# A hybrid encoder on one core: the DeltaNet solver's entry reordered, and the norms with spare matmuls, one later POOL unit and halved x transfers

## What is computed

```python
for i in range(DEPTH):                      # DEPTH = 2
    h = _rmsnorm(x, norm_mix[i])
    x = x + (_mixer_gdn if i == 0 else _mixer_ssd)(h, ...)
    x = x + _peer(_rmsnorm(x, norm_ffn[i]), peer_w_q[i], peer_keys[i], peer_u[i], peer_v[i])
return _rmsnorm(x, norm_final)
```

## Time and profile before

| | |
|---|---|
| median of 3 executions | 2225.3 us (2224.41 to 2226.25) |
| the profiled execution: time / span | 2224.22 us / 2222.3 us |
| PE busy | 2145.9 us, 97% of the span |
| DVE / ACT / POOL busy | 67% / 60% / 49% |
| mean granted PE clock | 0.986 |

### The profile page before, as it was taken

How to read it: one execution, slowest core, us unless ns; L and a number is a source line. 1 busy time by engine, 2 the same in 40 slices (tenths; PEclk the granted TensorE clock), 3 DMA queues, 4 the chain that set the end, 5 groups by cost and what they waited for, 6 DMA issues and landing times.

```text
span 2222.3 us, 46035 instructions
## 1 busy us (share of the span) xinstructions
PE 2145.9 (97%) x14384; PEld 1980.1 (89%) x14384; DVE 1488.0 (67%) x3206; ACT 1340.2 (60%) x2739; POOL 1080.7 (49%) x831
## 2 busy tenths in 40 slices
PE   7989799999999999999989998999999999999998
PEld 6979799999999988888888877999999999888886
DVE  5766419975666577777766662399666665777776
ACT  7755455568787544444466775555777875444444
POOL 6841579997667600000066457799866674000000
PEclk9999999999999999999999999999999999999999
DMA  5520245554444566666634225455544445666664
GB/s 170 163 66 1 95 152 171 170 169 150 137 141 142 168 195 191 194 193 191 196 117 159 86 86 171 159 173 161 180 139 137 140 142 174 194 190 196 191 193 145
DMA packets 93872, 343.66 MB, mean 155 GB/s; under 512 B 10688, under 2 KB 10752, under 8 KB 93152
## 3 DMA queue, kind: packets, MB, share of 16 engines
q1 hardware_dynamic: 92592, 338.21, 49.0%
q0 software_dynamic: 912, 4.07, 0.6%
q10 hardware_dynamic: 288, 0.34, 0.1%
HBM read 341.53 MB, written 1.05 MB: 154 GB/s over the span
## 4 chain that ended last, share of the span: by engine, by line
PE 83%; POOL 7%; issue 5%; DVE 2%; ACT 2%; DMA 1%; POOLq 0%; DVEq 0%; ACTq 0%
PE bank L361 81%; POOL w_lo L1796 7%; PE bank L526 1%; PE bank L381 0%; ACT w_hi L1408 0%; DMA small<-in_ssd_d 0%; DVE arena L882 0%; ACT arena L1408 0%; ACT arena L1434 0%; DVE arena L997 0%; DVE arena L1037 0%; DVE arena L1004 0%; DVE arena L933 0%; PE bank L727 0%; PE bank L450 0%
## 5 line engine op out<-in xcount | busy, mean ns | idle before, releaser
L1796 POOL TENSOR_TENSOR w_lo<-ring,w_hi 128x512 fp32r<-128x512 f32 x744 | 996.4, 1355 | 647.3 <-ACT w_hi L1408 635.5
L1408 ACT ACTIVATE w_hi<-ring 128x512 fp32r<-128x512 f32 x1280 | 802.7, 628 | 523.5 <-PE bank L361 521.8
L361 PE MATMUL bank<-hT_hi,w_hi 128*128 128x256 f32 x2688 | 780.2, 290 | 8.4 <-POOL w_lo L1796 6.4
L361 PE MATMUL bank<-hT_lo,w_hi 128*128 128x256 f32 x2688 | 761.5, 283 | 0.0
L361 PE MATMUL bank<-hT_hi,w_lo 128*128 128x256 f32 x2688 | 761.4, 283 | 0.0
L361 PEld LDWEIGHTS bank<-hT_hi,w_hi 128*128 128x128 f32 x2688 | 516.3, 192 | 19.3 <-POOL w_lo L1796 18.7
L361 PEld LDWEIGHTS bank<-hT_lo,w_hi 128*128 128x128 f32 x2688 | 516.8, 192 | 0.0
L361 PEld LDWEIGHTS bank<-hT_hi,w_lo 128*128 128x128 f32 x2688 | 516.0, 192 | 0.0
L908 DVE TENSOR_TENSOR w_lo<-ring,w_hi 128x512 fp32r<-128x512 f32 x536 | 378.4, 706 | 198.7 <-ACT w_hi L1408 191.3
L361 PE MATMUL bank<-w_hi,p_ag_hi 128*128 128x512 f32 x1024 | 398.4, 389 | 0.0
L361 PE MATMUL bank<-w_lo,p_ag_hi 128*128 128x512 f32 x1024 | 398.4, 389 | 0.0
(11 more groups left out here) (250 smaller groups left out, 2252.1 us busy)
## 6 DMA issues: line engine op xcount, KB each, us to landing
ring<-in_peer_u SPq DMA_DIRECT2D x256, 512.0 KB, 3.5
ring<-in_peer_v SPq DMA_DIRECT2D x256, 512.0 KB, 3.7
ring<-in_peer_wq SPq DMA_DIRECT2D x32, 512.0 KB, 3.5
ring<-in_gdn_qkv SPq DMA_DIRECT2D x24, 512.0 KB, 3.5
ring<-in_ssd_xbc SPq DMA_DIRECT2D x24, 512.0 KB, 3.5
ring<-in_ssd_z SPq DMA_DIRECT2D x16, 512.0 KB, 3.6
ring<-in_ssd_out SPq DMA_DIRECT2D x16, 512.0 KB, 3.5
ring<-in_gdn_z SPq DMA_DIRECT2D x8, 512.0 KB, 3.5
```

The lines of the kernel that those rows point to most:

```text
L361: return pe.matmul(o, w, r, start=first, stop=last)
L1408: return act.activation(o, i, ACT.Copy, scale=scale)
L1796: pool.tensor_tensor(w_part[1][:, s, :], ring[:, n % RING, hf * 512:(hf + 1) * 512], w_part[0][:, s, :].bitcast(F32), ALU.subtract).then_i ...
```

## The change

**Solver entry.** The backs move from banks 4 to 7 to banks 2 to 5. The second z half's units no longer stand behind heads 0 to 3: unit 0 stands ahead of the backs, unit 1 behind back 1, unit 2 behind head 5, unit 3 behind head 7. ACT splits two z units between the backs, and the two `go` units in solver steps 8 and 9; its copies of the finished z half move into step 4. POOL makes the rests of the two `go` units after its masks, not before them. DVE runs `extend(0)` behind head 3 and `extend(1)` behind head 5.

**Norms.** In `turn_h(i)` PE makes 18 matmuls of hT with itself into bank 3, whose result nobody reads, before it waits for the first pieces (three float32 matmuls of constants for i = 0). POOL makes the rest of one unit less ahead of the norms 1 and 3 (and of norm 2's unit 1) and waits for the last piece (`n_h`) before that unit; the load of the peer keys moves ahead of that wait. In norm 0 ACT loads the square root's table first.

**Transfers.** x comes in as two DMAs of one token block each, norm 0 takes its squares block by block, and the result goes out as two DMAs, each behind its own scaling.

```diff
@@ sync
-            sp.dma_start(x_sb[:, :, :], a["x"]).then_inc(x_loaded, 16)
+            for t in range(NT):
+                sp.dma_start(x_sb[:, t, :], a["x"][:, t, :]).then_inc(x_loaded[t], 16)
...
+            for t in range(NT):
+                sp.wait_ge(SEM["finished"], t + 1)
+                sp.dma_start(out[:, t, :], x_sb[:, t, :]).then_inc(SEM["stored"], 16)
@@ tensor
             def turn_h(i):
+                for e in range(KEEP_WARM if i else 3):
+                    if i:
+                        mm(PS[3][:, :], hT[0][:, 0, 0:P], hT[0][:, 0:2, :])
+                    else:
+                        mm(PS[3][:, :], ident, const[:, 0:4, :])
                 for b in range(4):
                     pe.wait_ge(n_h, 8 * i + 2 * (b + 1))
...
                 by_token(("gz", 0), 0, 2, 4)
+                pe.wait_ge(row_lo, 1)
+                pe.wait_ge(SEM["g_toksb"], 12)
+                by_token(("gz", 1), 6, 0, 1)
 
                 for gi in range(GH):
                     pe.wait_ge(SEM["g_qk"], gi // 2 + 1)
...
-                            last = pe.transpose(PS[4 + gi % 4][:, (2 * e + t) * P:(2 * e + t + 1) * P],
+                            last = pe.transpose(PS[2 + gi % 4][:, (2 * e + t) * P:(2 * e + t + 1) * P],
                                                 g_tok[:, t, 2 * gi + e, :], ident)
                     last.then_inc(SEM["g_backps"], 1)
+                    if gi == 1:
+                        by_token(("gz", 1), 6, 1, 2)
...
-                    if h < KD // 2:
-                        by_token(("gz", 1), 6, h, h + 1)
+                    if h in (5, 7):
+                        by_token(("gz", 1), 6, (h - 1) // 2, (h + 1) // 2)
@@ vector
-                for h in range(GH):
-                    system_rows(h)
-                dve.wait_ge(SEM["g_exps"], 2)
-                link(dve.tensor_scalar(g_egq, g_eg, P ** -0.5, None, ALU.mult))
...
-                for n in range(GB):
-                    extend(n)
+                for h in range(GH):
+                    system_rows(h)
+                    if h >= 3 and h % 2:
+                        extend((h - 3) // 2)
+                extend(GB - 1)
+                dve.wait_ge(SEM["g_exps"], 2)
+                link(dve.tensor_scalar(g_egq, g_eg, P ** -0.5, None, ALU.mult))
@@ scalar
-                if i:
-
-                    act.activation(n_idle, n_root, ACT.Sqrt)
+                if not i:
+                    act.wait_ge(root_primed, 1)
+                act.activation(n_idle, n_root, ACT.Sqrt)
...
+                    if gi in (3, 6):
+                        split(z + 6 + gi // 6)
...
-                    if h < 4:
-                        split(z + 6 + h)
-                    if h == 5:
-                        z_out(1, 6)
...
                     x_out(n)
+                    if n == GB:
+                        z_out(1, 6)
+                    if n in (2 * GB, 2 * GB + 1):
+                        split(z + n)
@@ gpsimd
             def early_experts(lyr, start):
 
-                rest_of_units(start + 2, tables[lyr] + 2)
+                pool.wait_ge(n_h, 16 * (lyr + 1))
+                rest_of_units(start + 1, tables[lyr] + 2)
...
-            rest_of_units(0, at[("go", 2)])
+            rest_of_units(0, at[("go", 0)])
             for b in range(GB):
                 pool.wait_ge(SEM["g_Ah"], 2 * (b + 1))
...
+            rest_of_units(at[("go", 0)], at[("go", 2)])
...
-            rest_of_units(at[("go", 2)], at[("pq", 0, 0)] + 2)
+            rest_of_units(at[("go", 2)], at[("pq", 0, 0)] + 1)
             load_keys(0)
             early_experts(0, at[("pq", 0, 0)])
```

More of the change, by code:

```diff
@@ L64 @@
 EARLY = 56
+KEEP_WARM = 18
 EXP_AT, TURN_AT = 36, 48
@@ L288, in hybrid_encoder @@
         mask = flat(p_ag[1][:, :, :], "s t")
-        x_loaded, small_loaded, gain_loaded = sem("x_loaded"), sem("small_loaded"), sem("gain_loaded")
+        x_loaded, small_loaded, gain_loaded = [sem(f"x{t}_loaded") for t in range(NT)], sem("small_loaded"), sem("gain_loaded")
+        root_primed = sem("root_primed")
         const_loaded = sem("const_loaded")
@@ L352, in _ @@
             sp.dma_start(last_gain, a["norm_final"].partition_broadcast(P)).then_inc(last_gain_loaded, 16)
-            sp.wait_ge(SEM["finished"], 1)
-            sp.dma_start(out, x_sb[:, :, :]).then_inc(SEM["stored"], 16)
-            sp.wait_ge(SEM["stored"], 16)
+            for t in range(NT):
+                sp.wait_ge(SEM["finished"], t + 1)
+                sp.dma_start(out[:, t, :], x_sb[:, t, :]).then_inc(SEM["stored"], 16)
+            sp.wait_ge(SEM["stored"], 16 * NT)
         @block.tensor
@@ L544, in z_step @@
                     pe.wait_ge(SEM["g_Y"], n - GB + 1)
+                    if n == GB:
+                        pe.wait_ge(SEM["g_zraw"], 2 * NT)
                     if n - 2 >= GB:
@@ L1384, in experts @@
                 residual(n3 - 1)
-            dve.wait_ge(x_loaded, 16)
+            dve.memset(n_root, 1.0).then_inc(root_primed, 1)
+            for t in range(NT):
+                dve.wait_ge(x_loaded[t], 16)
             norm(0)
@@ L1400, in _ @@
             for t in range(NT):
-                ins = dve.scalar_tensor_tensor(x_sb[:, t, :], x_sb[:, t, :], n_rstd[:, t:t + 1], last_gain, ALU.mult, ALU.mult)
-            ins.then_inc(SEM["finished"], 1)
+                dve.scalar_tensor_tensor(x_sb[:, t, :], x_sb[:, t, :], n_rstd[:, t:t + 1], last_gain, ALU.mult, ALU.mult
+                                         ).then_inc(SEM["finished"], 1)
         @block.scalar
@@ L1425, in norm_squares @@
             def norm_squares(i):
-                if i:
-                    act.activation(n_idle, n_root, ACT.Sqrt)
-                for hf in range(2):
-                    for t in range(NT):
-                        if i:
-                            act.wait_ge(x_added, 4 * (i - 1) + 2 * hf + t + 1)
-                        part = 2 * hf + t
-                        act.activation(h_junk[:, (part % 2) * 512:(part % 2 + 1) * 512], x_sb[:, t, hf * 512:(hf + 1) * 512], ACT.Square,
-                                       scale=D ** -0.5, accum_out=n_ss[:, hf, t:t + 1]).then_inc(n_sq, 1)
-                        if part >= 1:
-                            act.wait_ge(n_sq, 4 * i + part)
+                if not i:
+                    act.wait_ge(root_primed, 1)
+                act.activation(n_idle, n_root, ACT.Sqrt)
+                for part in range(4):
+                    hf, t = divmod(part, 2) if i else (part % 2, part // 2)
+                    if i:
+                        act.wait_ge(x_added, 4 * (i - 1) + part + 1)
+                    else:
+                        act.wait_ge(x_loaded[t], 16)
+                    act.activation(h_junk[:, (part % 2) * 512:(part % 2 + 1) * 512], x_sb[:, t, hf * 512:(hf + 1) * 512], ACT.Square,
+                                   scale=D ** -0.5, accum_out=n_ss[:, hf, t:t + 1]).then_inc(n_sq, 1)
+                    if part >= 1:
+                        act.wait_ge(n_sq, 4 * i + part)
                 act.wait_ge(n_mean, i + 1)
@@ L1441, in norm @@
             def norm(i):
-                if i == 0:
-                    act.wait_ge(x_loaded, 16)
                 norm_squares(i)
@@ L1524, in gdn @@
                     act.wait_ge(SEM["g_backps"], gi + 1)
-                    copy(g_feat[:, 2 * gi:2 * gi + 2, :], PS[4 + gi % 4][:, :].rearrange("p (e t) -> p e t", e=2)).then_inc(SEM["g_backsb"], 1)
+                    copy(g_feat[:, 2 * gi:2 * gi + 2, :], PS[2 + gi % 4][:, :].rearrange("p (e t) -> p e t", e=2)).then_inc(SEM["g_backsb"], 1)
+                    if gi in (3, 6):
+                        split(z + 6 + gi // 6)
                 for h in range(GH):
@@ L1851, in _ @@
             pool.wait_ge(lo_ready, 2 * at[("sx", 0)])
-            rest_of_units(at[("sx", 0)], at[("sx", 2)])
+            rest_of_units(at[("sx", 0)], at[("sx", 1)])
+            pool.wait_ge(n_h, 24)
+            rest_of_units(at[("sx", 1)], at[("sx", 2)])
             pool.wait_ge(s_wg_loaded, 16)
             pool.wait_ge(half_used, 2 * at[("sx", 0)])
-            pool.wait_ge(n_h, 24)
             split_gates(s_wg, s_wgs, SEM["s_wg_hi"], SEM["s_wg_lo"])
@@ L1884, in _ @@
             pool.wait_ge(lo_ready, 2 * at[("so", 2)])
-            rest_of_units(at[("so", 2)], at[("pq", 1, 0)] + 2)
+            rest_of_units(at[("so", 2)], at[("pq", 1, 0)] + 1)
             load_keys(1)
```

4 lines of the change are left out of this document (removed).

## The result

| | before | changed |
|---|---|---|
| median, us | 2224.86 (2221.82 to 2226.25, 4 runs) | 2202.31 (2201.32 to 2202.98, 4 runs) |
| span of the profiled execution, us | 2222.3 | 2200.1 |
| mean granted TensorE clock | 0.986 | 0.994 |
| PE busy, us | 2145.9 | 2152.3 |

The ratio is 0.9902, 95% interval 0.9889 to 0.9914: faster by 22.5 us by the medians, where 19.0 was forecast. PE is busy for longer by the matmuls that were added, and the span is shorter all the same.

What follows compares the result with a forecast made beforehand. PE was taken to bound the kernel, busy 97% of the span, so only its idle and half-clock time could be won. Terms 10.1 + 7.0 + 1.5 + 0.4 = 19.0 us gave a median of 2206.3 us, range 2202 to 2210.

Steps and rivals of the forecast that it cites:

- term 3: Start: spare matmuls shorten PE's rest, so the first projection avoids half speed; gain 1.5 us, ends -1 and 1.6.
- term 1: Three inner norms: spare matmuls keep the clock, POOL's moved unit frees DVE's pieces; gain 10.1 us, between 6 and 11.
- Every sign: Norms in the changed profile: transposes' wait under 0.5 us, pieces in 2.2 us, clock 1.00, 18 matmuls 0.23 us apart.
- rival (b): Norms: spare matmuls don't keep the clock or pieces stay slow; 1.5 to 2 us a norm, 2211.5 us; chance 0.1.
- rival (c): Norms: spare matmuls are dear, 0.9 us each; 16 us slower, 2241.6 us, deciding from 0.58 us each; chance 0.04.
- Rival (d): Stages behind the norms: what is won in front is waited for later; 2221 to 2229 us; chance 0.05.
- term 2: Solver's entry: moved z units and extends start the solver earlier; gain 7.0 us, low end 4, high end 9.5.
- Rival (a): Solver's entry gives little: half clock, ACT's splits delay head 0, extends wait; gain 2 to 4 us, 2209 to 2211; chance 0.2.
- The 1.1 us taken off for the clock: Solver's entry: deducted from a gain of 8.1 us for a clock that may fall behind PE's rests, leaving 7.0.
- Extends at 1.7 us beside POOL: Solver's entry: each level-0 extend between heads meets POOL's add and takes 1.7 us; about 0.85 us without any blocking.
- My -1 case: Start: low end, a loss of 1 us if the constants land 2 us late.
- term 4: End: the second block's store starts when the one store did before; gain 0.4 us, 0.3 to at most 1.3.

Runs made afterwards that it cites:

- e1: Changed kernel without its 3 x 18 spare matmuls in the inner norms; POOL's unit still waits behind the pieces: 2207.08 us, ratio 0.9928.
- e8: Changed kernel with 36 spare matmuls in each inner norm, not 18: 2214.6 us, ratio 0.9955.
- e4: Changed kernel with five more spare float32 matmuls of 256 columns behind the first norm's transposes: 2199.64 us, ratio 0.9896.
- e7: Changed kernel with x loaded in one transfer and the result stored in one, as before: 2202.76 us, ratio 0.9903.
- f10: Changed kernel with the added spare matmuls of both f9 and e4: 2199.05 us, ratio 0.9884.
- e6: Kernel before with only the level-0 extends moved between the heads: 2224.12 us, ratio 1.0004.
- e3: Changed kernel with neither the inner norms' spare matmuls nor POOL's later unit: 2212.83 us, ratio 0.9949.
- f12: Kernel before, no edit, profiled a second time: 2224.15 us (one run).
- f9: Changed kernel with more spare matmuls in the mixers (18 in the first; 12 and 9 in the second): 2199.11 us, ratio 0.9887.
- f11: Changed kernel, no edit, profiled a second time: 2202.75 us, ratio 0.9902.
- e2: Changed kernel with POOL's second unit again beside the pieces in all three norms; spare matmuls stay: 2210.54 us, ratio 0.9943.

## Why the prediction was right, point by point

The range held the time and the direction was right; the terms hold in part. To size them I take both profiles of either kernel, since one of before alone misplaces up to 2 us. The stage means sum to 21.7 us. There was luck in it: the 2202.3 us lie at the very edge of the forecast's own range, 2202 to 2210, and if term 3 had come true too, the time would have been near 2200.8, below it.

- **Norms (term 1): 10.1 forecast, 10.5 measured** (3.4, 3.6 and 3.5). Every sign came: no rest, pieces of 2.19 us, clock 1.00, 0.23 us apart. e1 shows what rival (b) gives without the clock, 1.3 to 1.7 us a norm, where it said 1.5 to 2. e8 prices a spare matmul at 0.22 us, so that rival (c), which needed 0.58, falls. Rival (d) falls too: the stages behind the norms keep their length in the table.
- **POOL's moved unit: hidden, as worked out.** By the Trainium skill (SBUF — State Buffer, Who interferes with whom) DVE and GpSimd exclude each other on the ports that they share. The trace agrees here, with 4.18 us beside POOL and 2.19 without.
- **Entry (term 2): 7.0 forecast, 8.4 measured** (7.6 between the first two profiles). The chain came within 0.5 us at most steps: 124.85 for 125.3, 147.87 for 148.3, the third step's transposes at 149.68 for 149.2, but for DVE's first rows, 126.99 for 126.4. Rival (a), with 2 to 4 us, falls. The 1.1 us taken off for the clock was nearly right for the changed kernel (its entry is 1.2 to 1.9 us longer than e4's, where the clock is 1.00 from the first head on). What was mis-sized is the side of before: its entry differs by 2.2 us between two profiles, by where the clock is low (last section), and I had measured from the better one.
- **Extends at 1.7 us beside POOL: 1.75 to 1.78**, and 1.11 for the one that POOL doesn't meet (the forecast's 0.85 for it was too low). Each of the three extends ends 0.97 to 0.99 us after POOL's add does, and so does the 2.11 us one of before. POOL's mask, which comes next, takes 1.80 to 1.82 us beside an extend and 1.16 alone.
- **Start (term 3): 1.5 forecast, none in either profile of the changed kernel. This step failed**: the matmuls "begin when the constants are in, at about 1.2 + 9.4 = 10.6 us", and from it "it rests now for under 1 us". The 9.4 was a duration of the kernel before, for a small transfer issued while x is on its way, and the same change halves x: it fell to 7.5. So PE rests 3.89 and 2.99 us; e7 puts the landing back to 9.4 and rests 1.33. Whether the clock then stays is a second question, and it isn't settled by the landing: five of the six other profiles with the changed start rest 1.74 to 2.81 us and take 86.6 us, the forecast time, and in these the clock rose later (last section). e4 and f10 rest 1.15 and 1.47 us, with matmuls nearer to the projection, and keep a clock that rose as early as in the changed kernel. My -1 case was for constants that land late; early ones were not thought of. Nor was it thought of that PE might run at half speed from its first matmul on, as it did in the second profile of before, without a fall behind the rest.
- **End (term 4): 0.4 forecast, 1.1 to 1.2 measured** (e7). The second store takes 2.7 us; I had read 3.6 off another transfer of 512 KB.
- **Not forecast: 1.1 us in the second mixer**, which the change doesn't touch, in the means (2.1 in the first pair). e6, where that mixer and its norm are as before, has 240.58, as the changed kernel has; e3, with the changed start and entry, has 241.96. The clock accounts for it. PE's 16 products there follow the same rest of 3.18 us in both profiles of before and take 6.71 us in the first, 5.52 in f12. The stretch at 0.50 around them lasts 6.8 us in the first and in e3, the two with 242 us, 3.4 us in the ten profiles with 240.1 to 240.6, and there is none in f9 and f10, with 239.6. What makes it the one or the other isn't settled.

The sum was 2.7 us short: term 3 too high by 1.5 in the changed kernel's two profiles, and terms 1, 2 and 4 too low by 0.4, 1.4 and 0.7, with the mixer's 1.1 and 0.6 in the expert stages and the first wait, which differ by chance. The parts moved against each other; it isn't a proof of each.

## What to carry to other kernels

Matmuls that nothing needs pay where the whole rest is known and ends in one wait, and they must reach up to the work behind it: three at the start brought nothing in the three profiles where PE then rested 2.9 us or more, and 1.5 us in the five where it rested less; with five more behind them the clock stayed both times. Ask of every duration that a sum takes over from the old trace whether the change itself moves what it competed with. Two edits that look alike in cost can need each other (spare matmuls and a free DVE; units moved away and extends put into their gap), so a part that wins nothing alone may still be half of the gain. Profile a kernel twice before a stage's difference under 2 us is put down to an edit.

## What the runs showed of the hardware

**At the start the clock has to rise first, and the clock column doesn't show that.** It reads 1.00 until the profile's first record of the clock. PE's rows and two windows of the second profile of before (f12; the clock is the third number from the end):

```profile
12.98 3.64 PE L381 MATMUL bank<-const,arena 128*128 128x128 f32 x16 [12.98 <-DVE arena L882]
18.79 0.58 PE L361 MATMUL bank<-hT_hi,w_hi 128*128 128x256 f32 x1 [2.16 <-POOL w_lo L1796]
```

```profile
19.00:22.00 3.00, 3.00 (x15) 3.00 (x16) 1.49 (x4) 0.58 (x3) 3.00 (x3) 1.00 0.23 35
22.00:25.00 3.00, 3.00 (x26) 3.00 (x26) 0.96 (x2) 1.55 (x4) 2.26 (x3) 1.00 0.80 283
```

Both windows say 1.00, but the first has 15 matmuls, as the changed kernel has 16 in 3 us at 0.51, and the second 26. The transposes stand 0.21 us apart from the first on, where the changed kernel has 0.11. So PE ran at the lower level (1.2 GHz) from its first matmul to 22.1 us, and nothing fell behind the rest. e6 shows the same up to 21.4. In the first profile of before the clock rose at 16.0, during the transposes, and fell at 19.5, behind a rest of 2.21 us. The start took 88.0 to 88.1 us in all three.

**The clock behind a rest.** In the eight profiles with the changed kernel's start the spare matmuls begin at the lower level too: their first records stand 0.85 us apart, those behind the rise 0.43. Where the clock rose at 11.7, 12.6 and 13.1 us (changed, f11, e8), it fell again, at 18.5 to 19.9, behind rests of 3.89, 2.99 and 2.90 us. Where it rose at 13.7 to 15.2, it stayed, behind rests of 1.74 to 2.81 us. An early rise makes the matmuls before the rest faster and so the rest longer, and these runs don't tell the two apart. e4 and f10 rose at 12.3 and 12.2 and kept the clock behind 1.15 and 1.47 us; e7 rose at 15.1 and kept it behind 1.33. A rest of 1.92 us kept it in e2's norms 1 and 2 and lost it in norm 3.

**One kernel, two profiles.** The way into the solver before, in the first profile and then in f12:

```profile
117.00:121.00 4.00, 2.73 (x19) 2.09 (x19) 1.94 (x2) 3.53 (x9) 0.00 (x0) 1.00 0.44 131
```

```profile
117.70:121.10 3.40, 3.16 (x15) 3.17 (x16) 1.32 (x2) 2.00 (x5) 0.00 (x0) 0.50 0.42 154
148.00:156.00 8.00, 4.38 (x20) 4.01 (x21) 6.26 (x5) 3.88 (x10) 2.80 (x2) 0.53 0.00 0
156.00:158.60 2.60, 2.60 (x14) 2.60 (x13) 0.73 (x2) 0.60 (x1) 0.00 (x0) 0.50 0.00 0
```

f12 has a stretch at 0.50 ahead of the heads that the first profile lacks, and its first solver transposes came at 150.92 instead of 149.64; the lower level then lasted to 158.7 instead of 156.0. Together its entry took 2.2 us longer. Norm 1 made up 1.4 us: there the lower level outlasted the start of the transposes by 2.9 us instead of 5.9. In the second mixer f12 is 1.8 us shorter; PE's first products there, in the first profile and in f12:

```profile
1204.62 6.71 PE L361 MATMUL bank<-arena 128*128 128x256 f32 x16 [3.18 <-ACT arena L1589]
```

```profile
1206.28 5.52 PE L361 MATMUL bank<-arena 128*128 128x256 f32 x16 [3.18 <-ACT arena L1589]
```

That one kernel's clock differs from execution to execution, the Trainium skill says too (TensorE: Matmul & The Clock Gate, Part 1: The HAM clock gate): the same kernel runs another number of matmuls at the lower clock from one execution to the next. The trace agrees, with the stages of the table, which trade up to 2.2 us at a span that is the same within 0.2 us.
